# Three SBUF areas of a two-block transformer kernel start 64 bytes lower

## The chip, the cores and the metric

The kernel runs on one core of a Trainium2 chip. The metric is the time of one execution on the device, in microseconds (us); lower is better. Three runs of the kernel before gave a median of 3033.0 us.

## The reference

Two transformer blocks of two layers each work on 512 tokens of width 1024, all in float32. The first block adds 256 context tokens; its first layer mixes global attention with a long convolution, its second windowed with neighbourhood attention. Each layer of the second block mixes three attentions (sparse, latent, forgetting), adds a cross attention to a memory, and ends in a 1024 to 4096 to 1024 network:

```
for l in range(DEPTH):
    y = hybrid_mixer(x, w_in[l], ...)                     # 3 attentions, gates, w_out
    x = layer_norm(DN_ALPHA * x + y, ln_g[l, 0], ln_b[l, 0])
    y = memory_cross_attention(x, mem, xa_w_q[l], xa_w_kv[l], xa_w_o[l])
    x = layer_norm(DN_ALPHA * x + y, ln_g[l, 1], ln_b[l, 1])
    y = jnp.square(jax.nn.relu(x @ mlp_w_up[l])) @ mlp_w_down[l]
    x = layer_norm(DN_ALPHA * x + y, ln_g[l, 2], ln_b[l, 2])
```

Most of the arithmetic is the product of the tokens with a weight matrix, layer after layer.

## The kernel before, in words

**Areas.** Each of the 128 partitions of SBUF is laid out by hand, in float32 elements, by the constants at L19 to L30. `CONST` holds small constants; `XR` holds X, the residual stream of six tiles of 1024 columns (and, while X is parked in memory, other tiles of the first block); `RAW` holds two slots of 2048 elements into which weights are loaded; `HL` holds two places for split weights, each of a high and a low part of 2048 elements; `BIG` to `END` holds everything else. The byte address of an element is the base plus four times its offset. The base is the first free byte rounded up to 32 (L98), 16,512, which is a multiple of 128; so an offset that is a multiple of 32 starts at 0 modulo 128 bytes. `XR`, `RAW`, `HL` and `BIG` all do. Inside the big area the tiles `h0_high`, `h0_low`, `h1_high`, `y0_*`, `y1_*`, `branch_*`, `mixed_*` and `hd*` also start at 0 modulo 128. One does not: `xT`, the transposed tokens of the second block, lies at `XT_HL = AREA + 17104`, that is 23,248 elements above `BIG`, and 4 x 23,248 = 92,992 bytes is 726.5 x 128: it starts at 64 modulo 128. All steps inside these tiles (over k, over tokens, over columns, between high and low) are multiples of 512 bytes, so every operand cut from a tile keeps the tile's start modulo 128. A float32 tile in the constants, `ka`, starts at 32 modulo 128: two of the four decay tables loaded at L416 go there and two to the big area at 0, and the matmuls at L2863 take their moving operand from it, where those of L1209 take theirs from tiles at 0. `h1_low` lies at `XR`.

**Weights.** Every weight goes through a list of chunks, mostly 1 MB (128 partitions of 8 x 256 elements). SP issues the loads (`sp_chunks`, L343 to L350), chunk i into RAW slot i modulo 2, once chunk i - 2 is no longer read. For most chunks ACT then writes the high part, the weight rounded to the matmul's narrower format, into HL (`act_split`, L295), and DVE subtracts that from the raw weight to give the low part (`dve_split`, L302); the profile calls the raw slot `S` and the split places `HL`. A chunk is split one or two ahead of its use (`take`, L319).

**Products.** A product of tokens and split weights is three matmuls per 128 rows of depth, high by high, high by low, low by high, all of type fp32r (`acc3`, L354 to L360; L664, L3680 and L3781 spell out the same three):

```
THREE = ((0, 0), (0, 1), (1, 0))
for i, (l, r) in enumerate(pairs):
    for j, (x, y) in enumerate(THREE):
        m = pe.matmul(dst, l[x], r[y], ...)
```

`l` is the stationary operand, which LDWEIGHTS loads (128 x 128); `r` is the moving one, 256 or 512 columns. The profile writes a matmul as out<-moving,stationary. Where tokens come out as rows, HL moves and the tokens (`h`, `y`, `xT`, `mixed`, `hd`) are stationary; where they come out as columns, HL is stationary and the tokens move. Of any three matmuls, two take the high tile of the tokens and one the low tile. Attention, the long convolution and the transposes use plain float32 matmuls, many of whose operands lie in the area of X or in HL while that is free.

**Order.** Each engine runs its program in the order written; PE starts a group of matmuls when the weights are split, its PSUM bank is free and the tokens are written. Between parts of the attention, PE is given weight products to do. In the last part of a second-block layer, `up` (L3737 on, HL stationary, xT moving, 512 columns, 24 matmuls to a group) and `down` (L3774 to L3784, HL moving, `hd` stationary) follow one another in long streams. xT itself is written by ACT (L2508) and DVE (L2514) out of PSUM.

Of the kernel before, what the change touches and what calls it, by code (L numbers as in the profile page):

```python
# [17 lines left out]


CONST = 0  # L20
XR = 3328
RAW = XR + 6144
HL = RAW + 4096
BIG = HL + 8192
END = 53200

T5_AT = BIG
GB_AT = T5_AT + 4096
# [66 lines left out]
def program(nc, D, out):  # L95
    pe, v, a, g, sp = nc.tensor, nc.vector, nc.scalar, nc.gpsimd, nc.sync
    base = -(-nc.sbuf_base // 32) * 32
    places = [(lo, hi, nc.alloc_sbuf_tensor_at(f"S{lo}", [128, hi - lo], F32, offset=base + 4 * lo))  # L98
              for lo, hi in ((CONST, RAW), (RAW, HL), (HL, BIG), (BIG, END))]
    PS = nc.alloc_psum_tensor("PS", [128, 8, 512], F32)  # L100
# [8 lines left out]
    def sb(off, *dims):  # L109
        lo, hi, place = [p for p in places if p[0] <= off][-1]  # L110
        assert off + math.prod(dims) <= hi
        x = place[:, off - lo:off - lo + math.prod(dims)]
        if len(dims) == 2:
            x = x.rearrange("p (a b) -> p a b", a=dims[0])
        if len(dims) == 3:
            x = x.rearrange("p (a b c) -> p a b c", a=dims[0], b=dims[1])
        return x
# [6 lines left out]
    def grid(base, n, *dims):  # L124
        s = math.prod(dims)
        return [sb(base + i * s, *dims) for i in range(n)]
# [240 lines left out]
    def cst(*dims):  # L367
        o = c_at["o"]
        c_at["o"] += math.prod(dims)
        assert c_at["o"] <= XR  # L370
        return sb(o, *dims)
# [19 lines left out]
    ka = cst(4, 256)  # L391
    X = sb(XR, 6, 1024)

# [1299 lines left out]
    def store_spectrum(x):  # L1693

        g.wait_ge(*x.done[-1])
        for k in range(x.nt):
# [6 lines left out]
    ALL = [(0, 512), (512, 256)]  # L1703
    adarow = sb(BIG + 31024, 256)
    ZR, ZI = sb(BIG, 4, 512), sb(BIG + 2048, 4, 512)
    zr, zi = sb(BIG + 4096, 2, 512), sb(BIG + 5120, 2, 512)
    T01 = [(sb(at, 4, 512), sb(at + 2048, 4, 512), sb(at + 4096, 2, 512), sb(at + 5120, 2, 512))
           for at in (BIG + 6144, BIG + 12288)]
    dftc = sb(BIG + 18432, 11, 128)
# [100 lines left out]
    UC = sb(BIG + 12288, 6, 1536)  # L1810
    QK = sb(XR, 6, 640)
    VV = sb(XR + 3840, 6, 128)
    g10 = sb(XR + 4608, 640)
    uct = grid(BIG + 27648, 2, 768)
# [2149 lines left out]
```

How the kernel before makes its waits and increments, by code:

```python
    def barrier():  # L138
        after = [mm.last(), vl.at, al.at, gl.at]
        for tok in after:
            pe.wait_ge(*tok)
        for tok in after:
            v.wait_ge(*tok)
        for tok in after:
            a.wait_ge(*tok)
        for tok in after:
            g.wait_ge(*tok)
        assert all(x.n == x.sent for x in (mm, dv, ac, gp))
        return after
# [137 lines left out]
    def act_split(i):  # L288
        x = chunks[i]
        a.wait_ge(*x["loaded"])
        if x["behind"] is not None:
            a.wait_ge(*hl_free[x["behind"]])
        for raw, high, low in x["parts"]:
            m = a.activation(high, raw, ACT.Copy)
        m.then_inc(*hi_made.up())
# [1 line left out]
    def dve_split(i):  # L298
        x = chunks[i]
        v.wait_ge(*x["hi"])
        for raw, high, low in x["parts"]:
            m = v.tensor_tensor(low, raw, high.bitcast(F32), ALU.subtract)
        m.then_inc(*lo_made.up())
# [39 lines left out]
    def sp_chunks():  # L343
        sp.wait_ge(*ld_last.all())
        for i, x in enumerate(chunks):
            if i > 1:
                sp.wait_ge(*raw_free[i - 2])
            for dst, src in zip(x["dsts"], x["srcs"]):
                sp.dma_start(dst, src).then_inc(raw_loaded[i % 2], 16)
# [60 lines left out]
        def pool():  # L411
            g.dma_start(cT, D["cT"]).then_inc(*ld_c.up())
            g.dma_start(ident, D["ident"]).then_inc(*ld_c.up())
            g.wait_ge(*ld_net.all())
            for n in range(4):
                g.dma_start(dec[n], D["decay1"][n * 128:n * 128 + 128, :]).then_inc(*ld_dec[n].up())
```

## Time and profile before

| | |
|---|---|
| median of three runs | 3033.0 us (3028.27 to 3035.07) |
| the profiled execution's own time | 3031.4 us |
| its span, first to last instruction | 3029.6 us |
| mean granted TensorE clock over the span | 0.985 |
| busy: PE / PEld / DVE / ACT / POOL | 2869.1 / 2228.4 / 1617.8 / 1026.5 / 442.7 us |

PE is the tensor engine's matmuls, PEld its weight loads (they overlap matmuls), DVE, ACT, POOL and SP the vector, scalar, general and sync engines. A group of instructions is written: line, engine, operation, out<-in, shapes, count, then busy us, mean ns of one, and the idle time of its engine just before. The mean ns of a matmul is its latency in a pipeline; the distance from one to the next, its pitch, is shorter.

### The profile page before, as it was taken

To read this page: it belongs to the slowest core of one execution; us is meant where nothing else is said; L and a number is where in the kernel's file an instruction comes from. 1 tells how busy PE (TensorE), PEld (TensorE's weight loads), DVE (VectorE), ACT (ScalarE), POOL (GpSimd) and SP (SyncE) were. 2 spreads that over 40 slices of the span, in tenths; PEclk is the share of its full clock that TensorE was granted. 3 is DMA by queue.
4 is the path that set the end of the run, shared out by engine and by line. 5 is a ranking of instruction groups with operands and counts; after the bars stand their busy time and mean duration, and the time that the engine had idled before them with its cause. 6 is when DMAs were issued, how large, how long until landed. Compare 5 with 4: busy or idle time off the path is not lost.

```text
span 3029.6 us, 40231 instructions
## 1 busy us (share of the span) xinstructions
PE 2869.1 (95%) x15815; PEld 2228.4 (74%) x15815; DVE 1617.8 (53%) x3155; ACT 1026.5 (34%) x1847; POOL 442.7 (15%) x401
## 2 busy tenths in 40 slices
PE   7899989999988899999999999999999999899998
PEld 3498865799964585666887788878566788778887
DVE  6735667845678646645245632435755334653344
ACT  2222244123156423544222432312454323332231
POOL 3300022320025321311020000000222011000000
PEclk9999999999999999999999999999899999999999
DMA  6533312042142142112323232334010323132321
GB/s 203 176 112 110 100 47 76 15 134 82 57 108 41 56 112 60 44 35 77 97 99 110 84 98 97 98 97 95 29 57 22 104 93 107 51 112 97 98 98 70
DMA packets 224932, 261.80 MB, mean 86 GB/s; under 512 B 12819, under 2 KB 187011, under 8 KB 224617
## 3 DMA queue, kind: packets, MB, share of 16 engines
q1 hardware_dynamic: 207328, 203.93, 21.8%
q0 software_dynamic: 12544, 45.08, 4.3%
q10 hardware_dynamic: 4872, 10.21, 1.5%
q8 instruction: 128, 2.10, 0.3%
q14 instruction: 60, 0.48, 0.0%
HBM read 245.04 MB, written 13.11 MB: 85 GB/s over the span
## 4 chain that ended last, share of the span: by engine, by line
PE 55%; DVE 8%; issue 2%; ACT 1%; DMA 1%; POOL 0%; SPq 0%; DVEq 0%; ACTq 0%; POOLq 0%
PE PS L359 31%; PE PS L3781 10%; PE PS L156 3%; PE PS L3680 2%; PE PS L1235 2%; PE PS L1224 2%; PE PS L1209 1%; DVE S L1264 1%; DVE HL L302 1%; DVE S L1292 1%; DVE S L2662 1%; PE PS L3441 1%; DMA S<-in_w_in 1%; DVE S L2658 1%; DVE S L1285 1%
## 5 line engine op out<-in xcount | busy, mean ns | idle before, releaser
L359 PE MATMUL PS<-xT,HL 128*128 128x512 f32 (+1 forms) x3552 | 790.3, 383 | 9.8 <-DVE xT L2514 4.7
L359 PEld LDWEIGHTS PS<-xT,HL 128*128 128x128 f32 x3552 | 642.8, 187 | 150.2 <-DVE xT L2514 5.4
L302 DVE TENSOR_TENSOR HL<-S,HL 128x2048 fp32r<-128x2048 f32 (+1 forms) x180 | 366.2, 2040 | 608.6 <-ACT HL L295 608.5
L295 ACT ACTIVATE HL<-S 128x2048 fp32r<-128x2048 f32 (+1 forms) x180 | 305.8, 1705 | 633.7 <-PE PS L359 286.6
L3781 PE MATMUL PS<-HL,hd 128*128 128x512 f32 x1536 | 351.7, 391 | 0.1
L3781 PEld LDWEIGHTS PS<-HL,hd 128*128 128x128 f32 x1536 | 289.1, 188 | 61.3 <-PE PS L3781 1.0
L1323 ACT ACTIVATE S<-S,S 128x256 f32<-128x256 f32 (+5 forms) x292 | 189.1, 648 | 182.9 <-DVE S L1264 175.6
L1358 POOL TENSOR_SCALAR S<-S,S 128x512 f32<-128x512 f32 (+4 forms) x104 | 179.6, 1727 | 380.3 <-DVE S L1279 220.3
L1224 PEld LDWEIGHTS PS<-S,S 128*128 128x128 f32 (+1 forms) x1048 | 114.4, 142 | 136.9 <-issue 47.2
L1224 PE MATMUL PS<-S,S 128*128 128x128 f32 (+1 forms) x1048 | 171.9, 291 | 35.7 <-DVE S L1292 19.3
L359 PE MATMUL PS<-h_high,HL 128*128 128x512 f32 (+1 forms) x768 | 201.2, 348 | 0.1
L1209 PE MATMUL PS<-S 64*128 64x256 f32 (+6 forms) x736 | 152.6, 487 | 20.5 <-DVE S L1264 15.9
L1264 DVE CUSTOM_DVE_ANT_0 S<-PS,S 128x512 f32<-128x512 f32 (+4 forms) x272 | 137.5, 535 | 54.1 <-PE PS L1209 29.9
L359 PE MATMUL PS<-HL,h_high 128*128 128x256 f32 x896 | 163.2, 285 | 2.6 <-DVE h_low L730 2.0
L156 PE MATMUL PS<-S,S 128*128 128x256 f32 (+2 forms) x704 | 158.5, 382 | 3.6 <-DVE xT L2514 1.5
L359 PEld LDWEIGHTS PS<-h_high,HL 128*128 128x128 f32 x768 | 135.2, 189 | 19.3 <-DVE HL L302 1.3
L156 PEld LDWEIGHTS PS<-S,S 128*128 128x128 f32 (+1 forms) x704 | 122.3, 190 | 35.0 <-issue 14.9
L1209 PEld LDWEIGHTS PS<-S 64*128 64x128 f32 (+1 forms) x736 | 69.9, 192 | 106.0 <-DVE S L1264 47.1
L359 PEld LDWEIGHTS PS<-HL,h_high 128*128 128x128 f32 x896 | 140.9, 194 | 3.2 <-DVE h_low L730 2.4
L359 PE MATMUL PS<-h_low,HL 128*128 128x512 f32 (+1 forms) x384 | 132.5, 345 | 0.0
L1235 PE MATMUL PS<-S 128*64 128x512 f32 (+4 forms) x580 | 130.2, 518 | 0.7 <-ACT S L1345 0.5
L359 PE MATMUL PS<-HL,h_low 128*128 128x256 f32 x448 | 127.5, 285 | 0.0
(413 smaller groups left out, 3917.1 us busy)
## 6 DMA issues: line engine op xcount, KB each, us to landing
S<-in_mlp_w_up SPq DMA_DIRECT2D x32, 1024.0 KB, 5.4
S<-in_mlp_w_down SPq DMA_DIRECT2D x32, 1024.0 KB, 5.0
S<-in_w_in SPq DMA_DIRECT2D x28, 1024.0 KB, 5.9
S<-in_w_ada SPq DMA_DIRECT2D x24, 1024.0 KB, 5.7
S<-in_w_gate SPq DMA_DIRECT2D x24, 1024.0 KB, 5.2
S<-in_w_in SPq DMA_DIRECT2D x36, 512.0 KB, 5.2
S<-in_w_mix_out SPq DMA_DIRECT2D x8, 1024.0 KB, 5.2
spectra<-S POOLq DMA_DIRECT2D x24, 256.0 KB, 4.8
```

Of the source, the lines that this page charges most:

```text
L156: m = pe.matmul(dst, l, r, start=(i == 0), stop=(i == n - 1))
L295: m = a.activation(high, raw, ACT.Copy)
L302: m = v.tensor_tensor(low, raw, high.bitcast(F32), ALU.subtract)
L359: m = pe.matmul(dst, l[x], r[y], start=(i == 0 and j == 0), stop=(i == n - 1 and j == 2))
L1209: m = pe.matmul(scores_of(n, i, h)[:, c0:c0 + nn], lr[h][0], lr[h][1], start=True, stop=True)
L1224: m = pe.transpose(PS[0:nk, b, q * 128:q * 128 + 128], j["P"][h][q][:, pcol(q):pcol(q) + nk], ident[:, :])
L1235: m = pe.matmul(PS[h * 64:h * 64 + 64, 7, q0 * 128:q1 * 128], vals[h], PT[tr[n, i, h][2]][0:nk, q0 * 128:q1 * 128], start=(i == 0 and j["f ...
L1264: x = v.tensor_tensor_reduce(out=shaped(Pq[:, c0:c1], bias[h]), in0=shaped(ps[:, c0:c1], bias[h]), in1=bias[h], scale=1.0, scalar=m if pla ...
L1323: x = a.activation(Pq[:, c0:c1], Pq[:, c0:c1], ACT.Exp, bias=m, scale=-1.0, accum_out=st[:, k, h, i:i + 1])
L1358: g.tensor_scalar(x, x, j["st"][:, 2, 1, i:i + 1], None, ALU.mult).then_inc(*gl.event())
L3680: m = pe.matmul(PS[:, t * 2 + h, :], mixed[x][:, part * 4 + k, t * 128:t * 128 + 128], w[y][:, k, :], start=(part == 0 and k == 0 and q == ...
L3781: m = pe.matmul(PS[:, t * 2 + h, :], hd[x][:, r * 8 + part * 4 + k, t * 128:t * 128 + 128], w[y][:, k, :], start=(r == 0 and part == 0 and ...
```

## The change

The area of X starts 16 elements (64 bytes) lower, and RAW and HL with it, since their offsets are counted from it. The gap that this leaves is put between HL and BIG, so BIG and all above it stay where they were. X, the raw slots and HL then start at 64 modulo 128 bytes, as does what else is cut from `XR`, `RAW` and `HL` (`h1_low` among it); xT was there already; the other tiles of the big area stay at 0. No instruction is added, removed or moved.

```diff
 CONST = 0
-XR = 3328
+XR = 3312
 RAW = XR + 6144
 HL = RAW + 4096
-BIG = HL + 8192
+BIG = HL + 8208
 END = 53200
```

## Rows read from the trace of the kernel before

**Rows 1.** The page, part 1: busy us (share of the span) and instructions of each engine.

```profile
PE 2869.1 (95%) x15815; PEld 2228.4 (74%) x15815; DVE 1617.8 (53%) x3155; ACT 1026.5 (34%) x1847; POOL 442.7 (15%) x401
```

**Rows 2.** By windows: stretch, us, busy (x) of PE, PEld, DVE, ACT, POOL; clock; DMA.

```profile
200.00:400.00 200.00, 200.00 (x1306) 173.13 (x1305) 106.83 (x198) 54.95 (x79) 0.00 (x0) 1.00 0.34 106
1704.00:2030.00 326.00, 325.13 (x1463) 269.18 (x1464) 119.71 (x105) 95.64 (x96) 0.82 (x2) 1.00 0.31 103
```

**Rows 3.** The chain of work that ended last: shares of the span by line.

```profile
by line: PE PS L359 31.0%; PE PS L3781 10.3%; PE PS L156 3.3%; PE PS L3680 2.3%; PE PS L1235 1.8%; PE PS L1224 1.6%; issue 1.6%; PE PS L1209 1.4%; DVE S L1264 1.3%; DVE HL L302 0.8%; DVE S L1292 0.7%; DVE S L2662 0.6%; PE PS L3441 0.6%; DMA
```

**Rows 4.** Groups by line and form, PE, window 712 to 820 us.

```profile
L359 PE MATMUL PS<-HL,h_high 128*128 128x256 f32 x601 | 108.3, 283 | 0.0
L359 PE MATMUL PS<-HL,h_low 128*128 128x256 f32 x301 | 85.2, 283 | 0.0
```

**Rows 5.** The same view, window 2232 to 2253 us.

```profile
L359 PE MATMUL PS<-HL,xT 128*128 128x256 f32 x188 | 21.6, 276 | 0.8 <-PE PS L1235 0.8
```

**Rows 6.** The same view, window 2068 to 2075 us.

```profile
L359 PE MATMUL PS<-xT,HL 128*128 128x256 f32 x62 | 7.5, 279 | 0.0
```

**Rows 7.** The same view, window 1791 to 1877 us.

```profile
L3781 PE MATMUL PS<-HL,hd 128*128 128x512 f32 x380 | 86.3, 389 | 0.0
```

**Rows 8.** The same view, window 1880 to 1965 us.

```profile
L359 PE MATMUL PS<-xT,HL 128*128 128x512 f32 x373 | 85.5, 391 | 0.0
```

**Rows 9.** Groups by line and form, the whole span: the fp32r matmuls.

```profile
L359 PE MATMUL PS<-xT,HL 128*128 128x512 f32 x3216 | 743.8, 392 | 8.5 <-DVE xT L2514 4.7 <-DVE S L3794 1.7 <-ACT S L1345 0.8
L3781 PE MATMUL PS<-HL,hd 128*128 128x512 f32 x1536 | 351.7, 391 | 0.1
L359 PE MATMUL PS<-HL,h_high 128*128 128x256 f32 x896 | 163.2, 285 | 2.6 <-DVE h_low L730 2.0 <-PE PS L359 0.6
L359 PE MATMUL PS<-h_high,HL 128*128 128x512 f32 x448 | 144.2, 394 | 0.1
L359 PE MATMUL PS<-HL,xT 128*128 128x256 f32 x768 | 89.4, 277 | 1.7 <-PE PS L1235 1.7
L359 PE MATMUL PS<-HL,y_high 128*128 128x256 f32 x480 | 87.1, 284 | 0.0
L359 PE MATMUL PS<-branch_high,HL 128*128 128x512 f32 x256 | 82.1, 392 | 0.0
L3680 PE MATMUL PS<-HL,mixed_high 128*128 128x512 f32 x256 | 81.8, 401 | 1.3 <-ACT S L3661 1.1
L359 PE MATMUL PS<-h_high,HL 128*128 128x256 f32 x320 | 60.7, 283 | 0.0
L359 PE MATMUL PS<-xT,HL 128*128 128x256 f32 x288 | 35.4, 281 | 1.3 <-DVE HL L302 1.3
```

**Rows 10.** Groups by line and form, the whole span: ACT and DVE reading PSUM.

```profile
L2514 DVE TENSOR_TENSOR xT<-PS,xT 128x512 fp32r<-128x512 f32 x48 | 30.7, 682 | 5.6 <-ACT xT L2508 5.6
L2101 DVE TENSOR_TENSOR S<-PS,S 128x512 f32<-128x512 f32 x48 | 30.1, 683 | 9.9 <-ACT S L2117 7.8 <-POOL S L2110 1.7
L2508 ACT ACTIVATE xT<-PS 128x512 fp32r<-128x512 f32 x48 | 26.2, 591 | 20.7 <-PE PS L2502 20.4
L3580 ACT ACTIVATE S<-PS 128x512 f32<-128x512 f32 x48 | 24.8, 593 | 0.0
```

**Rows 11.** Line 416, four loads of decay tables: DMA from issue to landing.

```profile
DMA to landing us min/median/max: 5.9/6.1/6.4
```

**Rows 12.** Line 350, SP's weight loads: who waited for them (us, times).

```profile
  ACT HL L295: 70.5, 9
```

**Rows 13.** Groups by line and form, the whole span: two plain float32 groups.

```profile
L1209 PE MATMUL PS<-S 64*128 64x256 f32 x304 | 50.1, 411 | 3.4 <-DVE S L1264 1.8 <-ACT S L1089 1.6
L2863 PE MATMUL PS<-S,S 64*128 64x256 f32 x64 | 9.1, 401 | 1.8 <-DVE S L2603 1.0 <-ACT S L2612 0.8
```

**Rows 14.** Groups by line and form, the whole span: the split of a weight chunk.

```profile
L302 DVE TENSOR_TENSOR HL<-S,HL 128x2048 fp32r<-128x2048 f32 x138 | 316.4, 2293 | 538.7 <-ACT HL L295 538.6
L295 ACT ACTIVATE HL<-S 128x2048 fp32r<-128x2048 f32 x138 | 263.6, 1910 | 529.4 <-PE PS L3781 244.4 <-PE PS L359 191.4 <-DMA S<-in_w_out 34.5
```

## The prediction

> **What bounds the kernel now.** The order of reading is: the page's busy shares, the windows, the chain, then the matmul groups one form at a time. PE is busy 95% of the span [rows 1], and the windows show where that is solid: 200.00 of 200 us in the weight products of the first layer, 325.13 of 326 us in the 1024 to 4096 to 1024 network, with DVE under 54% and ACT under 30% in both [rows 2]. The chain that ended last goes through the fp32r matmuls: lines 359, 3781 and 3680 hold 43.6% of the span, while DVE's split line holds 0.8% [rows 3]. So the bound is the pitch of fp32r matmuls, and the change can only matter by altering it, since it adds and removes nothing.
>
> The pitch can be had from a window inside one stream. A matmul is counted if any of its own time touches the window, so count x pitch = window + mean duration. With weights moving past first-block tokens, both at 0 modulo 128, 256 columns: (108 + 0.283) / 902 = 120.0 ns [rows 4]. With weights (0) moving past a stationary xT (64): (21 + 0.276) / 188 = 113.2 ns [rows 5]. With xT (64) moving past stationary weights (0): (7 + 0.279) / 62 = 117.4 ns [rows 6]. At 512 columns, both at 0: (86 + 0.389) / 380 = 227.3 ns [rows 7]; xT (64) moving: (85 + 0.391) / 373 = 228.9 ns [rows 8]. One matmul more or less in the count is 0.6 ns in rows 5 and about 2 ns in rows 6. The shapes are equal; the operand's tile, and so its start, is what differs.
>
> **The steps.** From these rows, starting at 64 instead of 0 moves the pitch by -6.8 ns for a stationary operand (113.2 - 120.0), by +1.6 ns for a moving one of 512 columns (228.9 - 227.3) and by -2.6 ns for one of 256 (117.4 - 120.0). The change moves HL from 0 to 64, and HL is one operand of every fp32r matmul. Counts are in rows 9; six more groups, with the low token tiles, have half the count of the row of their high tile.
>
> (a) HL stationary, big-area tokens moving: 448 x 1.5 + 256 x 1.5 = 1056 of 512 columns and 320 x 1.5 = 480 of 256 [rows 9]. This becomes the pairing of rows 5. 1536 x -6.8 = -10.4 us. The step was seen at 256 columns only; if the 512 keep their pitch, it is 480 x -6.8 = -3.3 us. I take -10.4, the only row with a stationary operand at 64.
>
> (b) HL moving, big-area tokens stationary: 1536 + 256 x 1.5 = 1920 of 512 columns, (896 + 480) x 1.5 = 2064 of 256 [rows 9]. This becomes the pairing of rows 6 and 8. 1920 x 1.6 = +3.1 us, 2064 x -2.6 = -5.4 us: -2.3 us. If not the operand's own start counted but only that the two differ, the step would be that of rows 5: 3984 x -6.8 = -27.1 us.
>
> (c) HL stationary, xT moving, the largest group: 3216 of 512 columns and 288 of 256 [rows 9]. Both at 64 stands nowhere in the trace. One end: equal starts behave as equal starts do at 0, so 228.9 goes to 227.3 and 117.4 to 120.0: 3216 x -1.6 + 288 x 2.6 = -4.4 us. Other end: the stationary step comes on top: 3504 x -6.8 = -23.8 us. No row is nearer to one end, so I take the middle, -14.1 us.
>
> (d) HL moving, xT stationary: 768 of 256 columns [rows 9], both at 64 again. Ends: 768 x +6.8 = +5.2 us (back to 120.0) and 768 x -2.6 = -2.0 us. Middle +1.6 us.
>
> (e) Not fp32r: 1834 of the plain float32 matmul records have an operand in the moved areas (counted in the program). The nearest pair of rows has the moving operand at 32 and at 0: 401 and 411 ns a matmul [rows 13]. I take nothing; at 6.8 ns each way it would be 12 us, which I don't put into the range in full.
>
> (f) ACT and DVE on moved tiles: into xT at 64 they take 591 and 682 ns, elsewhere at 0 593 and 683 ns [rows 10]. Nothing. The split itself, 2.3 us on DVE after 1.9 us on ACT [rows 14], is covered by the 11 us that a chunk's 48 matmuls take (48 x 228.9 ns).
>
> (g) Loads into raw slots: the four decay loads, two to starts at 32 and two at 0, landed in 5.9 to 6.4 us [rows 11]. Waits of ACT for weights sum to 70.5 us, nine of them [rows 12]; 0.5 us more on each would be 4.5 us, mostly under PE's work in progress. I take nothing, and keep 0 to +4.5 for the range. SP's queue issues as before; it waits for free slots, which come sooner if PE is faster.
>
> Sum: -10.4 - 2.3 - 14.1 + 1.6 = -25.2 us of pitch. What reaches the end is what lies on the chain: line 3781 is busy 351.7 us [rows 9] and holds 10.3% of 3029.6 = 312 us of the chain [rows 3], 0.89. So -22 us. The profiled execution took 3031.4 us, 1.6 below the median of 3033.0; taken off the median, 3011 us.
>
> **What is late next.** Nothing waits in place of PE: in the network a chunk needs 4.2 us of ACT and DVE in 11 us. In the attention parts a shorter filler may end before DVE does, which is the 11% that I leave out.
>
> **A rule against this.** Rows 4 to 6 show one shape at three pitches, 120.0, 113.2 and 117.4 ns. The Trainium skill ("SBUF — State Buffer", Specifications (TRN2)) says that SBUF has 16-byte cachelines and that full bandwidth needs two hits in a line; by it a start at 64 is as good as one at 0, both being multiples of 16, and the sum would be nothing. The same page of the Trainium skill ("Who interferes with whom") gives the moving operand and the weight load independent read ports. The trace doesn't agree so far, unless something else about xT makes the difference.
>
> **Rivals.**
> 1. Equal starts are equal: (c) and (d) at their first ends. -10.4 - 2.3 - 4.4 + 5.2 = -11.9, x 0.89 = -11: 3022 us. For it: if two reads disturb each other, only their difference should count. Against: 113.2 and 117.4 ns, the same difference with the roles exchanged, aren't equal.
> 2. Each operand counts by itself: second ends. -10.4 - 2.3 - 23.8 - 2.0 = -38.5, x 0.89 = -34: 2999 us. For it, as against 1: the two different steps. Against: nothing shows that they add.
> 3. No effect: xT's pitch comes from its place or its layout and not from the start modulo 128; HL at 64 changes nothing. 3033 us. The cacheline rule of the Trainium skill ("SBUF — State Buffer", Specifications (TRN2)) would give this time. Against: the moving xT and the stationary xT both differ from the tiles at 0.
> 4. Slower: two reads that both start at 64 collide more than any pairing shown. Its place is (c) and (d); its price, taken as the largest step shown: 3216 x 6.8 + 768 x 6.8 = +27.1; with -10.4 and -2.3 left, +14.4, x 0.89 = +13: 3046 us. It decides once (c)'s pitch at 512 columns is above about 231 ns: then 3216 x 2.3 + 5.2 of (d) eats the 12.7 saved.
>
> **How the numbers follow.** A measurement of this kernel can tell about 0.2%, 6 us. Chances: forecast, (c) and (d) between their ends and the time between rivals 1 and 2, 0.33; rival 1, 0.22; rival 2, 0.18; rival 3, 0.14; rival 4, 0.13. Faster by over 0.2%: 0.33 + 0.22 + 0.18 = 0.73; within: 0.14; slower: 0.13. The range leaves out rival 4 and the far ends of (b) and (e): from 2993 (rival 2 less 6 us for a part of (b)'s other end) to 3036 (rival 3 plus most of (g)). The likeliest time is 3011.
>
> **What would show it.** In the changed kernel's trace: (a) line 359 with `branch_high`, `h_high` moving, pitch 220 instead of 227 at 512 columns, 113 instead of 120 at 256; (b) line 3781 at 229 instead of 227, line 359 with `h`, `y` stationary at 117; (c) xT moving between 222 and 227; (d) xT stationary between 111 and 120. The same groups' busy times fall with them. The forecast is wrong if (c) stays at 229 or rises, if (a) stays at 227 and 120, or if the pitches fall and DVE waits grow by as much in the attention parts.

## The result and the profile after

The changed kernel took 3050.1 us (median of 6 runs, 3046.3 to 3051.8) against 3033.1 us (6 runs) for the kernel before on the same chip: a ratio of 1.0058, 95% interval 1.0045 to 1.0071. It is slower by 17 us, where 22 us less were forecast, and outside the range given. Its profiled execution took 3051.2 us with a span of 3049.4 us, 19.8 us more than the one before in both.

The page, part 1, of the changed kernel:

```profile
PE 2887.1 (95%) x15815; PEld 2224.4 (73%) x15815; DVE 1617.0 (53%) x3155; ACT 1026.2 (34%) x1847; POOL 441.9 (14%) x401
```

PE is busy 18.0 us longer than in [rows 1], with the same instructions; DVE, ACT and POOL do the same in the same time. By windows, the network of a second-block layer (columns as in [rows 2]) is as solid as before, at a granted clock of 1.00 both times, but the stretch that holds the same 1463 matmuls is 333 us long instead of 326:

```profile
1705.30:2038.30 333.00, 332.12 (x1463) 269.98 (x1464) 119.68 (x105) 95.62 (x96) 0.83 (x2) 1.00 0.31 101
```

The order of the instructions is the same on every engine. So in the network no wait was added and no clock was lost; the fp32r matmuls take longer to follow one another. Groups by line and form, PE, whole span, of the changed kernel:

```profile
L359 PE MATMUL PS<-xT,HL 128*128 128x512 f32 x3216 | 754.9, 395 | 9.2 <-DVE xT L2514 4.7 <-DVE S L3794 1.7 <-DVE HL L302 1.0
L3781 PE MATMUL PS<-HL,hd 128*128 128x512 f32 x1536 | 361.0, 396 | 0.1
L359 PE MATMUL PS<-HL,h_high 128*128 128x256 f32 x896 | 158.6, 281 | 3.0 <-DVE h_low L730 2.3 <-PE PS L359 0.6
L359 PE MATMUL PS<-h_high,HL 128*128 128x512 f32 x448 | 144.7, 397 | 0.0
L359 PE MATMUL PS<-HL,xT 128*128 128x256 f32 x768 | 93.2, 282 | 1.7 <-PE PS L1235 1.7
L359 PE MATMUL PS<-HL,y_high 128*128 128x256 f32 x480 | 84.3, 281 | 2.6 <-DVE HL L302 2.6
L359 PE MATMUL PS<-xT,HL 128*128 128x256 f32 x288 | 35.7, 283 | 1.2 <-DVE HL L302 1.2
```

Against [rows 9] the two large groups of 512 columns rise, xT moving from 743.8 to 754.9 us and `hd` stationary from 351.7 to 361.0, and xT stationary from 89.4 to 93.2. The first block's groups of 256 columns fall (`h_high` stationary 163.2 to 158.6, `y_high` 87.1 to 84.3). The same view in four windows of the changed kernel (1795 to 1880, 1895 to 1965, 2242 to 2260, 735 to 800 us):

```profile
L3781 PE MATMUL PS<-HL,hd 128*128 128x512 f32 x366 | 85.6, 396 | 0.0
...
L359 PE MATMUL PS<-xT,HL 128*128 128x512 f32 x303 | 70.6, 395 | 0.0
...
L359 PE MATMUL PS<-HL,xT 128*128 128x256 f32 x154 | 18.4, 281 | 0.0
...
L359 PE MATMUL PS<-HL,h_high 128*128 128x256 f32 x370 | 65.4, 282 | 0.0
L359 PE MATMUL PS<-HL,h_low 128*128 128x256 f32 x185 | 52.0, 281 | 0.0
```

Window plus mean, over count, gives the pitch as in the prediction: `hd` (85 + 0.396) / 366 = 233.3 ns where [rows 7] gave 227.3; xT moving (70 + 0.395) / 303 = 232.3 where [rows 8] gave 228.9; xT stationary (18 + 0.281) / 154 = 118.7 where [rows 5] gave 113.2; `h` stationary (65 + 0.282) / 555 = 117.6 where [rows 4] gave 120.0.

Where along the span the time goes is read from the starts of two lines, the first write of xT (L2508, the start of the second block) and the `down` product (L3781). Single lines, of the kernel before and then of the changed one; the last two numbers ahead of the semicolon are the first and last start in us:

```profile
L2508 ACT ACTIVATE xT<-PS x48: 578/592/600, 1085.4 to 2671.2; 128x512 fp32r<-128x512 f32 x48
...
L3781 PE MATMUL PS<-HL,hd x1536: 387/389/628, 1789.9 to 3019.7; 128*128 128x512 f32 x192
```

```profile
L2508 ACT ACTIVATE xT<-PS x48: 578/592/600, 1080.7 to 2684.1; 128x512 fp32r<-128x512 f32 x48
...
L3781 PE MATMUL PS<-HL,hd x1536: 388/394/775, 1792.4 to 3040.1; 128*128 128x512 f32 x192
```

So the first block is 4.7 us ahead, the first `down` already 2.5 us late, and the last 20.4 us late: the first block gained and the second lost some 25 us. The largest wait that was added, 2.6 us for a split, lies at the end of the first block (the `y_high` line above).

### The profile page after: what moved, and what is told of

The parts are those of the page before. It is cut to its first block, busy times and chain, and to the rows that moved or that the text cites. A ratio compares the mean times of both kernels' runs of the same rounds, so it can differ in the third digit from the quotient of the medians.

```text
span 3049.4 us, 40231 instructions
## 1 busy us (share of the span) xinstructions
PE 2887.1 (95%) x15815; PEld 2224.4 (73%) x15815; DVE 1617.0 (53%) x3155; ACT 1026.2 (34%) x1847; POOL 441.9 (14%) x401
## 4 chain that ended last, share of the span: by engine, by line
PE 56%; DVE 8%; issue 2%; ACT 1%; POOL 0%; DMA 0%; DVEq 0%; SPq 0%; ACTq 0%; POOLq 0%
PE PS L359 32%; PE PS L3781 10%; PE PS L156 3%; PE PS L3680 2%; PE PS L1235 2%; PE PS L1224 2%; PE PS L1209 2%; DVE S L1264 1%; DVE HL L302 1%; DVE S L1292 1%; DVE S L2662 1%; PE PS L3441 1%; ACT HL L295 1%; DVE S L2658 1%; DVE S L1285 1%
## 5 line engine op out<-in xcount | busy, mean ns | idle before, releaser
L359 PE MATMUL PS<-xT,HL 128*128 128x512 f32 (+1 forms) x3552 | 801.6, 386 | 10.4 <-DVE xT L2514 4.7
L3781 PE MATMUL PS<-HL,hd 128*128 128x512 f32 x1536 | 361.0, 396 | 0.1
L3781 PEld LDWEIGHTS PS<-HL,hd 128*128 128x128 f32 x1536 | 289.2, 189 | 70.4 <-PE PS L3781 1.0
L1209 PE MATMUL PS<-S 64*128 64x256 f32 (+6 forms) x736 | 155.7, 492 | 21.4 <-DVE S L1264 15.5
L359 PE MATMUL PS<-HL,h_high 128*128 128x256 f32 x896 | 158.6, 281 | 3.0 <-DVE h_low L730 2.3
L1209 PEld LDWEIGHTS PS<-S 64*128 64x128 f32 (+1 forms) x736 | 70.6, 193 | 107.5 <-DVE S L1264 46.4
L1235 PE MATMUL PS<-S 128*64 128x512 f32 (+4 forms) x580 | 128.1, 512 | 0.7 <-ACT S L1345 0.5
```

What stands on the lines that cost most here:

```text
L359: m = pe.matmul(dst, l[x], r[y], start=(i == 0 and j == 0), stop=(i == n - 1 and j == 2))
L1209: m = pe.matmul(scores_of(n, i, h)[:, c0:c0 + nn], lr[h][0], lr[h][1], start=True, stop=True)
L1235: m = pe.matmul(PS[h * 64:h * 64 + 64, 7, q0 * 128:q1 * 128], vals[h], PT[tr[n, i, h][2]][0:nk, q0 * 128:q1 * 128], start=(i == 0 and j["f ...
L3781: m = pe.matmul(PS[:, t * 2 + h, :], hd[x][:, r * 8 + part * 4 + k, t * 128:t * 128 + 128], w[y][:, k, :], start=(r == 0 and part == 0 and ...
```

## The experiments

**How pitches are given.** Beside the rows, pitches below are means of the distance from one matmul's start to the next of the same stream (distances over 250 ns left out), from the start times in each trace. Runs 4 and 8 are one execution each. I call **lead** the start of the stationary operand less the start of the moving one, in bytes, modulo 256. In the kernel before, the lead is 0 for HL with every big-area tile, 192 for xT moving past HL, 64 for HL moving past xT. The change makes them 64 for HL moving past a big-area tile, 192 for HL stationary, 128 for both pairings with xT. One tile is apart: `h1_low` lies in X's area and moves with HL, so its lead stays 0 while that of `h1_high` changes.

**Theory and rival.** After the result the theory was that the pitch goes by the lead. The rival was the prediction's own premise, that each operand's start modulo 128 counts by itself, with loads or X at 64 as a further suspect.

**1. Everything 64 bytes up.** The kernel before with the base of the layout 64 bytes higher, so that X, RAW, HL and the big area all start at 64 modulo 128:

```diff
-END = 53200
+END = 53192
-XT_HL = AREA + 17104
+XT_HL = AREA + 16992
-    base = -(-nc.sbuf_base // 32) * 32
+    base = -(-nc.sbuf_base // 32) * 32 + 64
```

> Every tile starts 64 bytes higher than before (the base is 64 higher; xT, which has no room above, goes 448 bytes lower, which is 64 higher modulo 512), so every difference between two starts stays what it was modulo 512 and every tile's own start changes. Pair theory (the pitch of an fp32r matmul goes by the difference of its operands' starts): time of before, 3033 us within 0.2%; line 3781 at 227 ns, xT moving at 229 ns, xT stationary at 114 ns. Own-start theory (each operand's start counts by itself): HL, hd and branch now at 64, so line 3781 moves off 227 ns, and the time goes up by 10 us or more. Load theory (X or raw slots at 64 cost the time): 3050 us, as in the change.

Measured: 3045.1 us against 3030.8, ratio 1.0042 (1.0028 to 1.0056). The expectation had an arithmetic slip: xT's offset was lowered by 448 bytes, so with the base it came down 384 bytes against HL's 64 up, and its lead is not as before but 128, as in the changed kernel. That makes the run a mixture, and a useful one. Groups, whole span, of this run:

```profile
L359 PE MATMUL PS<-xT,HL 128*128 128x512 f32 x3216 | 757.5, 396 | 9.5 <-DVE xT L2514 4.7 <-DVE S L3794 1.7 <-DVE HL L302 1.3
L3781 PE MATMUL PS<-HL,hd 128*128 128x512 f32 x1536 | 351.6, 391 | 0.1
L359 PE MATMUL PS<-HL,xT 128*128 128x256 f32 x768 | 93.2, 282 | 1.7 <-PE PS L1235 1.7
```

HL and `hd` both start at 64 with a lead of 0, and keep 351.6 us [rows 9: 351.7], 226.8 ns: where the two start by themselves does not matter. xT moving, lead 128, takes 757.5 us, 232.8 ns, and xT stationary 93.2 us, as in the changed kernel. Those two pairings alone cost 3216 x 3.8 + 768 x 4.9 = 16 us, and the run lost 14.

**2. X and the raw slots alone.** HL stays, X and RAW go to 64:

```diff
-XR = 3328
+XR = 3312
-HL = RAW + 4096
+HL = RAW + 4112
```

> X and the raw slots at 64 as in the change, HL at 0 as before (the 64 bytes of gap lie between the raw slots and HL). Pair theory and own-start theory: only HL matters, 3033 us within 0.2%, all fp32r pitches as before. Load theory: 3050 us with the pitches of before.

Measured: 3030.2 us, ratio 0.9996 (0.9987 to 1.0005). Groups, whole span, of this run:

```profile
L359 PE MATMUL PS<-xT,HL 128*128 128x512 f32 x3216 | 743.8, 392 | 9.7 <-DVE xT L2514 4.7 <-DVE S L3794 1.7 <-DVE HL L302 1.5
L3781 PE MATMUL PS<-HL,hd 128*128 128x512 f32 x1536 | 350.0, 389 | 0.1
```

Both stand as in [rows 9]. So the place of X and of the raw slots, and with it the loads, the splits' reads and the float32 matmuls on X, costs nothing that can be measured; the loss comes with HL's move. One part of the expectation failed, that all pitches stay: `h1_low` moved with X while HL did not, and from the start times the matmuls with `h1` go from 227.4 to 229.0 ns at 512 columns and from 120.1 to 117.9 at 256, some 2 us less in all, which the time can't show.

**3. The second block's tiles along with HL.** The changed kernel with the second block's tiles, xT among them, 64 bytes lower too; four places of the first block that were counted from the same constant are written out so that they stay:

```diff
-T5_AT = BIG
+T5_AT = BIG - 16
-              for lo, hi in ((CONST, RAW), (RAW, HL), (HL, BIG), (BIG, END))]
+              for lo, hi in ((CONST, RAW), (RAW, HL), (HL, T5_AT), (T5_AT, END))]
...
-    gates1 = sb(AREA + 12800, 1024)
+    gates1 = sb(BIG + 18944, 1024)
...
```

> The change, and the second block's tiles (T5 table, gains, hd, branch, mixed, xT, scratch) 64 bytes lower too, with HL; the first block's tiles h, y0, y1 stay, 64 above HL. Pair theory: from about 1090 us on, every pitch as before (227, 229, 114 ns); what the changed kernel gained by 834 us, some 7.7 us, stays: about 3025 us, 0.3% under before. Own-start theory: HL at 64 with hd and branch at 64 is no pairing seen yet; line 3781 not at 227 ns. Load theory: 3050 us.

Measured: 3025.3 us, ratio 0.9980 (0.9971 to 0.9989). Groups, whole span, then the first write of xT, of this run:

```profile
L359 PE MATMUL PS<-xT,HL 128*128 128x512 f32 x3216 | 743.8, 392 | 9.7 <-DVE xT L2514 4.7 <-DVE S L3794 1.7 <-DVE HL L302 1.5
L3781 PE MATMUL PS<-HL,hd 128*128 128x512 f32 x1536 | 351.3, 390 | 0.1
L359 PE MATMUL PS<-HL,xT 128*128 128x256 f32 x768 | 90.0, 278 | 1.7 <-PE PS L1235 1.7
L359 PE MATMUL PS<-HL,y_high 128*128 128x256 f32 x480 | 83.2, 278 | 0.1
```

```profile
L2508 ACT ACTIVATE xT<-PS x48: 577/592/599, 1076.9 to 2662.9; 128x512 fp32r<-128x512 f32 x48
```

The second block is back at the kernel before ([rows 9]: 743.8, 351.7, 89.4) although every operand there starts elsewhere than before, and the first block, 8.5 us ahead at the first write of xT (1085.4 before), keeps its gain: `y_high` 83.2 us against 87.1. The size of that gain differs between runs whose weights and first-block tokens lie alike: 8.5 us here, 4.7 in the changed kernel, 1.7 and 4.5 in runs 5 and 7. The loss lies in the second block's leads.

**4. A map of the pitch.** The whole computation is left out: fp32r streams of 72 matmuls run from two areas, with the stationary and the moving operand at chosen starts, one source line a stream.

> Leaves the whole computation out: it copies x to the output and runs 32 streams of 72 fp32r matmuls (high-high, high-low, low-high, 8 steps of depth, three groups), 512 columns and then 256, with the moving tile at 0 and at 64 and the stationary one at 0, 64, ... 448 modulo 512; one source line each. Pair theory: a stream's pitch is the same for moving 0, stationary s as for moving 64, stationary s + 64, and differs with s; at 512 columns about 227 ns for equal starts and about 233 ns for the stationary 64 above the moving; at 256 columns 120 for equal starts and 113 to 118 for 64 above. Own-start theory: it goes with s modulo 128 alone, and moving to 64 shifts all streams by one step.

Groups by line and form of this run (L51 to L54: 512 columns, lead 0, 64, 128, 192; L67 to L69: 256 columns, lead 0, 64, 128; L77: 256 columns, lead 64 with both operands 64 bytes further):

```profile
L51 PE MATMUL PS<-mv,st 128*128 128x512 f32 x72 | 16.5, 389 | 0.0
L52 PE MATMUL PS<-mv,st 128*128 128x512 f32 x72 | 17.0, 396 | 0.0
L53 PE MATMUL PS<-mv,st 128*128 128x512 f32 x72 | 16.9, 394 | 0.0
L54 PE MATMUL PS<-mv,st 128*128 128x512 f32 x72 | 16.6, 391 | 0.0
L67 PE MATMUL PS<-mv,st 128*128 128x256 f32 x72 | 8.8, 283 | 0.0
L68 PE MATMUL PS<-mv,st 128*128 128x256 f32 x72 | 8.6, 281 | 0.0
L69 PE MATMUL PS<-mv,st 128*128 128x256 f32 x72 | 8.7, 281 | 0.0
L77 PE MATMUL PS<-mv,st 128*128 128x256 f32 x72 | 8.3, 276 | 0.0
```

A stream without gaps has (busy - mean) / 71 as its pitch, to 0.7 ns: 226.9, 233.9, 232.5 and 228.3 for the first four. From the start times, over all 32 streams:

| pitch, ns | lead 0 | 64 | 128 | 192 |
|---|---|---|---|---|
| 512 columns, moving at 0 | 226.7 | 233.4 | 232.4 | 228.9 |
| the same, stationary 256 bytes further | 226.7 | 233.4 | 232.4 | 228.9 |
| 512 columns, moving at 64 | 226.8 | 233.4 | 232.4 | 228.9 |
| 256 columns, moving at 0 | 119.9 | 117.8 | 118.7 | 117.8 |
| 256 columns, moving at 64 | 120.0 | 113.4 | 118.6 | 117.8 |

At 512 columns the lead is all that counts in these streams, with period 256 in what was tried, and the four values are those of the kernels' long streams. At 256 columns a lead of 64 has two pitches, taken up in run 8.

In the map the high and the low tiles of a stream have the same lead. Where they differ, the map doesn't give the pitch: `h1` moving in the changed kernel has lead 192 for the high tile and 0 for the low one, so by the map at most 228.9 ns. Its rows there, window 828 to 857 us:

```profile
L359 PE MATMUL PS<-h_high,HL 128*128 128x512 f32 x84 | 26.4, 396 | 0.0
L359 PE MATMUL PS<-h_low,HL 128*128 128x512 f32 x42 | 16.6, 395 | 0.0
```

That is (29 + 0.396) / 126 = 233.3 ns. In run 2, with leads 0 and 64, the mean by the map would be 228.9 ns, and 229.0 was measured.

**5. xT put back against HL.** The changed kernel with xT 64 bytes lower, so that xT's pairs have their old leads and only the big area's pairs keep the new ones:

```diff
-XT_HL = AREA + 17104
+XT_HL = AREA + 17088
```

> The changed kernel with xT moved 64 bytes lower too, so that the differences between HL's pieces and xT's slots are again those of the kernel before (192 modulo 256 where xT moves, 64 where it is stationary), while the pairs of HL with the big area stay as the change made them. Theory of the difference of starts modulo 256: the xT-moving matmuls go back from 232.5 to about 229 ns, the xT-stationary ones from 119.6 to 113 to 116 ns, the HL-moving ones against hd stay at 233.3 ns; of the change's loss that takes about 3216 x 3.5 ns + 768 x 4 ns = 14 us away, giving about 3036 us, within 8 us of that. Rival, that each operand's own start counts (64 modulo 128 slow for HL): HL's start is the same as in the changed kernel, so 3050 us, with xT-moving matmuls still at 232 ns.

Measured: 3037.4 us against 3031.7, ratio 1.0024 (1.0014 to 1.0034). Groups, whole span, of this run:

```profile
L359 PE MATMUL PS<-xT,HL 128*128 128x512 f32 x3216 | 743.5, 392 | 9.7 <-DVE xT L2514 4.7 <-DVE S L3794 1.7 <-DVE HL L302 1.5
L3781 PE MATMUL PS<-HL,hd 128*128 128x512 f32 x1536 | 360.9, 395 | 0.1
L359 PE MATMUL PS<-HL,xT 128*128 128x256 f32 x768 | 90.4, 279 | 1.7 <-PE PS L1235 1.7
```

HL's start is the changed kernel's, yet xT moving is at 743.5 us (228.9 ns) and xT stationary at 90.4, while `hd` keeps the slow 360.9 (233.3 ns). From 1.0058 to 1.0024 is 10 us, for the two xT pairings; from 1.0024 to run 3's 0.9980 another 13 us, of which 9.6 are `hd` by the rows (360.9 to 351.3). The own-start rival wanted 3050 us here, and falls.

**6. xT on HL's residue in the kernel before.** The same line as in run 5, in the kernel before: lead 0 in every pair.

> The kernel before with only xT moved, 64 bytes lower, onto HL's residue (difference 0 modulo 256 in every pair). Theory of the difference: xT-moving matmuls of 512 columns go from 229.0 to 226.8 ns (about 3216 x 2.2 = 7 us less), xT-stationary ones of 256 columns from 113.4 to about 120 ns (768 x 6 = 4.6 us more): about 3030.5 us, a ratio near 0.999, with these two pitches in the rows. Own-start rival: xT goes from 64 to 0 modulo 128, where the own starts of the kernel before are all at 0 in the 226.8 ns pairs: no loss anywhere, 3021 to 3026 us, and 256-column matmuls stay near 113 to 116 ns.

Measured: 3028.5 us, ratio 0.9993 (0.9983 to 1.0003). Groups, whole span, of this run:

```profile
L359 PE MATMUL PS<-xT,HL 128*128 128x512 f32 x3216 | 737.0, 390 | 8.6 <-DVE xT L2514 4.7 <-DVE S L3794 1.7 <-ACT S L1345 0.8
L359 PE MATMUL PS<-HL,xT 128*128 128x256 f32 x768 | 94.1, 284 | 1.7 <-PE PS L1235 1.7
```

xT moving falls to 737.0 us (226.9 ns) and xT stationary rises to 94.1 (120.9 ns), the two terms that were expected; together they are within what can be told from no change.

**7. Run 3 with xT at a lead of 0.** Both edits of runs 3 and 5.

> The run second_along with xT 64 bytes lower besides, on HL's residue. Theory of the difference: hd pairs 226.8 ns as there, xT-moving 512-column matmuls 226.8 instead of 229.0 ns (7 us less), xT-stationary 256-column ones about 120 instead of 115.5 ns (3.5 us more): about 3022 us, a ratio near 0.997. Own-start rival: xT and HL both at 64 modulo 128 should be slow as in the changed kernel (232 ns): about 3036 us.

Measured: 3022.8 us against 3031.7, ratio 0.9969 (0.9960 to 0.9979), the fastest of all. Groups, whole span, of this run:

```profile
L359 PE MATMUL PS<-xT,HL 128*128 128x512 f32 x3216 | 736.8, 390 | 9.8 <-DVE xT L2514 4.7 <-DVE S L3794 1.7 <-DVE HL L302 1.7
L3781 PE MATMUL PS<-HL,hd 128*128 128x512 f32 x1536 | 349.9, 389 | 0.1
L359 PE MATMUL PS<-HL,xT 128*128 128x256 f32 x768 | 94.1, 284 | 1.7 <-PE PS L1235 1.7
```

All 512-column streams of the second block are at lead 0 (`hd` 226.7, xT 226.9 ns); the first block keeps the changed kernel's leads. Against run 3 the intervals overlap, so that this last step is a gain is shown by the rows only.

**8. The two pitches at lead 64, and small leads.** The whole computation is left out again.

> The whole computation is left out: x is copied to the output, and 24 streams of fp32r matmuls (72 each, the first 192) run from two areas of SBUF, one source line per stream. Lines 60 to 69: 256 columns, differences of starts 64, 64 (both operands 64 further), 0 and again 64 back to back; lines 71 to 79: such streams each behind a wait, so that each starts afresh; lines 82 to 88: 512 columns at differences of 4, 8, 16, 32, 48, 64 and 96 bytes. Theory that the pitch is set by the difference alone: all 256-column streams at 64 the same, 113.4 or 117.8 ns. Rival, that the phase in which a stream enters matters: 113.4 and 117.8 ns both occur at difference 64, and a stream keeps the one in which it began until a wait. For the fine differences: if what counts is a 64-byte unit, 4 to 48 bytes give 226.7 ns and 64 gives 233.4 ns; if it is gradual, they lie between.

Groups by line and form of this run. L60, L66 and L71 use the same operands (lead 64, moving at 0), L61, L67 and L73 the same 64 bytes further; L71 and L73 begin behind a wait. L82, L83, L84 and L88 are 512 columns at leads of 4, 8, 16 and 96 bytes:

```profile
L60 PE MATMUL PS<-mv,st 128*128 128x256 f32 x72 | 8.6, 281 | 0.0
L66 PE MATMUL PS<-mv,st 128*128 128x256 f32 x72 | 8.3, 276 | 0.0
L71 PE MATMUL PS<-mv,st 128*128 128x256 f32 x72 | 8.4, 278 | 0.3 <-ACT X L56 0.3
L61 PE MATMUL PS<-mv,st 128*128 128x256 f32 x72 | 8.3, 276 | 0.0
L67 PE MATMUL PS<-mv,st 128*128 128x256 f32 x72 | 8.6, 281 | 0.0
L73 PE MATMUL PS<-mv,st 128*128 128x256 f32 x72 | 8.4, 277 | 0.3 <-ACT X L56 0.3
L82 PE MATMUL PS<-mv,st 128*128 128x512 f32 x72 | 16.9, 394 | 0.0
L83 PE MATMUL PS<-mv,st 128*128 128x512 f32 x72 | 16.8, 393 | 0.0
L84 PE MATMUL PS<-mv,st 128*128 128x512 f32 x72 | 17.0, 396 | 0.0
L88 PE MATMUL PS<-mv,st 128*128 128x512 f32 x72 | 17.0, 396 | 0.0
```

L60 and L66 are one stream run twice, 8.6 and 8.3 us; from the start times 117.8 and 113.6 ns. L61 and L67 swap likewise, 113.5 and 117.7. Each stream keeps its pitch to its end. The four lead-64 streams behind a wait all settle at 113. So at 256 columns and lead 64 the starts alone don't decide between two pitches. Since only what ran before differs in the program, history is the likely cause, but the run doesn't show what in it. Expected was that a stream changes only at a wait; it changed where one stream followed another directly, too. The small leads went as neither theory said: 4 bytes give 232.4 ns, 8 give 230.7, 16, 32, 48 and 64 give 233.3 to 233.4, 96 gives 234.2. Not a 64-byte unit, and not gradual.

## Why the prediction was wrong

**What held.** The bound: the order on PE is the same in both traces, so the distances between starts can be compared one by one; they add 20.0 us, of which 19.7 stand in front of fp32r matmuls. Also (f): xT's writes take 591 and 682 ns and the split 1911 and 2293 ns after, as in [rows 10, 14]. And (g): decay loads land in 5.9 to 6.5 us, ACT's waits for weights sum to 56.2 us (nine) against 70.5 [rows 11, 12], and run 2 shows no price. (e) was small: of the plain float32 lines, L1209 is busy 3.1 us longer than before, L2863 0.9 us longer and L1235 2.0 us shorter, and the distances in front of all that is not fp32r add 0.4 us.

**What failed first.** The premise of "The steps", that a start of 64 instead of 0 moves the pitch by a step that belongs to the operand. Rows 4 to 8 hold leads 0 and 192 at 512 columns and 0, 64 and 192 at 256; no row of the kernel before shows 64 or 128 at 512 columns, and those are what the change brought to the long streams. Counting starts modulo 128 also hid that "both at 64" is not equal: HL and xT were then 128 bytes apart modulo 256. By steps, with pitches before and after from the start times:

- (a) -10.4 forecast. HL stationary got lead 192, not the 64 of [rows 5] that it was priced by. 512 columns: `branch` 228.7 to 229.3 ns, `h0` 228.5 to 229.2; `h1`, whose low tile moved and whose high tile did not, 227.4 to 233.3, which the leads don't explain (run 4). 256 columns: 119.7 to 117.2. With 384, 480, 192 and 480 matmuls: +0.2 + 0.4 + 1.1 - 1.2 = +0.5 us.
- (b) -2.3 forecast. The step for 512 columns, +1.6 ns, came from a row with lead 192; lead 64 costs `hd` 6.5 (226.8 to 233.3) and `mixed` 5.9: 1536 x 6.5 + 384 x 5.9 = +12.2 us. The pairing was that of [rows 5], lead 64, and not that of [rows 6, 8], lead 192. The 256-column part, whose count also left out the 192 matmuls of L664, came out below forecast at about -8 us (`y0` 120.0 to 113.4, `h1` 120.5 to 118.3, `h0` 125.1 to 118.4, short pauses included; `y1` about as before). Together +4.2. The other end that the step named, -27 if only the difference counts, had the right idea and the wrong price: it carried -6.8 from 256 to 512 columns.
- (c) -14.1 forecast. 229.0 to 232.5 at 512 columns, 119.6 to 120.5 at 256: 3216 x 3.5 + 288 x 0.9 = +11.5 us, outside both ends.
- (d) +1.6 forecast, end +5.2. 114.7 to 119.6: 768 x 4.9 = +3.8 us.

Sum: 0.5 + 4.2 + 11.5 + 3.8 = +20.0 us, against 19.8 between the profiled executions and 17 between the medians. That the first two agree so well is in part luck: single terms differ from what the starts give by up to 3 us, through pauses and the added wait, and these cancel. Whether the factor of 0.89 from the chain was needed can't be told: with it the sum is 17.8. Runs 5 and 3 take away (c) with (d) and then, mostly, the second block's part of (b), at 10 and 13 us.

**The rivals.** Rival 4 had the right side and the right place for over half the loss, (c) and (d), and its point of decision was passed: (c) came to 232.5, above 231. Its time of 3046 is near, but by compensating errors: 6.8 ns on (c) was twice too much, and (a) and (b) weren't savings. Its reason, that two reads both start at 64, falls with runs 1 and 7, where HL with `hd` and HL with xT both start at 64 and keep 226.8 and 226.9 ns. Rival 1's thought, that only the difference counts, is the right one; the argument against it, that 113.2 and 117.4 ns belong to the same difference with the roles exchanged, fails because the lead has a sign, 64 and 192. Its equal pair exists in run 6, and there (c) and (d) come to 226.9 and 120.9 ns, near its own ends of 227.3 and 120.0. Rival 2 falls with run 5, rival 3 with the result. The Trainium skill ("SBUF — State Buffer", Specifications (TRN2)) gives SBUF cachelines of 16 bytes, by which, read as the prediction read it, no lead in multiples of 64 bytes should matter; at 512 columns the runs show 226.7 to 233.4 ns over such leads.

**What stays open.** Why the lead matters; what sets which of two pitches a 256-column stream takes; and what the pitch goes by where the tiles of a stream have different leads, as with `h1`. Nor can the runs tell whether the moving operand meets the load of its own weights or of the next ones, since in all streams of the map both lie alike.

## What to carry to other kernels

In a kernel bound by fp32r matmuls, look at the distance of the two operands' starts, not at the alignment of each: give the long 512-column streams equal starts modulo 256 bytes, with the high and the low tiles alike, and leave distances to the 256-column streams, which were slowest at equal starts. The best layout tried was worth 0.3% here. Before a price is carried from one pair of tiles to another, write down for both the lead and the shape; where no row of the trace has the new combination, a stream of a few dozen matmuls at that lead, measured by itself, prices it. A move of one area changes every pair that it is part of, so a move that helps one stage is made with the tiles of the other stages along (run 7: 0.9969).

## What the runs showed that was not expected

- Streams of equal shape and type differ by up to 7.5 ns a matmul in 227 through the operands' distance alone (lead 0 against 96 bytes, runs 4 and 8), and four bytes are enough for 5.7 of it.
- The order turns round with the shape: a lead of 0 is the fastest tried at 512 columns (226.7 ns) and, of the multiples of 64, the slowest at 256 (120 ns).
- At 256 columns and lead 64 the same instructions on the same addresses ran at 113.6 or 117.8 ns within one execution, steadily over a whole stream. The kernels show it too: `y0` ran at 113.4 ns in the changed kernel and at 117.8 in run 5, with the same starts.
- A stream needs some matmuls to settle behind one of another lead. In the kernel before, `branch` (lead 0, at 1484 us) follows xT (lead 192): its first ten distances are 224 to 236 ns, all after them 226 to 227. In run 6, where xT has lead 0 too, they are 226 to 227 from the first on. So a short stream's mean is not its lead's pitch.
